# Differential attention's outputs normed by tokens inside its turns, the last layer's splits moved into the last eight turns, and silu by exponential and logarithm

## What is computed

```python
q, gate, q_mem, g_mem = split(rms_norm(x, pre) @ w_in)        # 768, 768, 256, 256 columns
k, v = split(rms_norm(x, kv_norm) @ w_kv)
# 6 pairs of heads, 8 tiles of 128 queries; keys up to the tile's end
p = softmax(q @ k.T / 8 - slope * dist)                        # two maps of each pair
o = (p[0] - lam * p[1]) @ v                                    # 128 features a pair
o = rms_norm(o, subln) * (1 - lam_init)                        # over the 128 features
y = concat(o * silu(gate), memory_attention(q_mem) * silu(g_mem)) @ w_out
x = x + rms_norm(y, post)
```

## Time and profile before

| | us |
|---|---|
| three runs | 3353.6, 3353.5, 3343.42 (median 3353.5) |
| the profiled execution | 3344.59, span 3343.3 |
| PE busy | 2864.3 (86%) |
| DVE busy | 1715.0 (51%) |
| ACT busy | 986.0 (29%) |
| POOL busy | 686.9 (21%) |

### The profile page before, as it was taken

How to read it: one execution, slowest core, us unless ns; L and a number is a source line. 1 busy time by engine, 2 the same in 40 slices (tenths; PEclk the granted TensorE clock), 3 DMA queues, 4 the chain that set the end, 5 groups by cost and what they waited for, 6 DMA issues and landing times.

```text
span 3343.3 us, 49988 instructions
## 1 busy us (share of the span) xinstructions
PE 2864.3 (86%) x20746; PEld 2296.5 (69%) x20746; DVE 1715.0 (51%) x3034; ACT 986.0 (29%) x1803; POOL 686.9 (21%) x531
## 2 busy tenths in 40 slices
PE   7978878699999999689999867777748899999767
PEld 6765667588888888567888646666627678766545
DVE  3425555544444444666554157777654433377634
ACT  3224444311111111633221211111143222255543
POOL 2112233211011110262111012222212211122123
PEclk9988999899999999899999968998979899999978
DMA  3111032011111111113112100000032201111222
GB/s 105 45 51 39 14 100 65 26 58 50 45 51 51 45 51 50 39 57 94 45 38 64 55 1 3 3 3 3 3 113 76 92 29 44 34 33 35 79 82 76
DMA packets 196450, 162.46 MB, mean 49 GB/s; under 512 B 5200, under 2 KB 173818, under 8 KB 195458
## 3 DMA queue, kind: packets, MB, share of 16 engines
q1 hardware_dynamic: 196226, 159.26, 15.1%
HBM read 137.19 MB, written 22.05 MB: 48 GB/s over the span
## 4 chain that ended last, share of the span: by engine, by line
PE 70%; DVE 16%; ACT 6%; issue 4%; POOL 2%; DMA 2%; SPq 0%; POOLq 0%; DVEq 0%; ACTq 0%
PE ps L721 15%; PE ps L723 14%; PE ps L722 14%; PE ps L2267 5%; PE ps L1836 3%; PE ps L1760 3%; DVE r L686 2%; PE ps L1462 1%; PE ps L1464 1%; PE ps L1463 1%; PE ps L773 1%; ACT r L681 1%; PE ps L1827 1%; PE ps L775 1%; PE ps L774 1%
## 5 line engine op out<-in xcount | busy, mean ns | idle before, releaser
L721 PE MATMUL ps<-r,r 128*128 128x512 f32 (+1 forms) x2304 | 939.7, 408 | 145.5 <-DVE r L686 118.5
L722 PE MATMUL ps<-r,r 128*128 128x512 f32 (+1 forms) x2304 | 911.1, 395 | 0.0
L723 PE MATMUL ps<-r,r 128*128 128x512 f32 (+1 forms) x2304 | 910.6, 395 | 0.0
L721 PEld LDWEIGHTS ps<-r,r 128*128 128x128 f32 x2304 | 444.6, 193 | 280.7 <-DVE r L686 132.1
L667 POOL TENSOR_TENSOR sb<-sb 128x1024 f32<-128x1024 f32 x138 | 281.6, 2046 | 1350.7 <-DMA sb<-in_w_ffn_up 483.5
L722 PEld LDWEIGHTS ps<-r,r 128*128 128x128 f32 x2304 | 445.3, 193 | 93.2 <-issue 6.2
L723 PEld LDWEIGHTS ps<-r,r 128*128 128x128 f32 x2304 | 443.3, 192 | 94.9
L2267 PE MATMUL ps<-sb 64*64 64x64 f32 (+2 forms) x8832 | 299.6, 226 | 120.0 <-DVE sb L2515 31.4
L2267 PEld LDWEIGHTS ps<-sb 64*64 64x64 f32 (+1 forms) x8832 | 278.9, 135 | 150.4 <-issue 100.1
L686 DVE TENSOR_TENSOR r<-sb,r 128x1024 fp32r<-128x1024 f32 x198 | 273.9, 1391 | 190.9 <-ACT r L681 190.5
L681 ACT CAST r<-sb 128x1024 fp32r<-128x1024 f32 x198 | 204.9, 1043 | 229.0 <-POOL sb L667 228.9
(11 more groups left out here) (276 smaller groups left out, 3602.1 us busy)
## 6 DMA issues: line engine op xcount, KB each, us to landing
sb<-in_w_out SPq DMA_DIRECT2D x36, 512.0 KB, 4.0
sb<-in_a_w_in SPq DMA_DIRECT2D x29, 512.0 KB, 4.0
sb<-in_w_ffn_gate SPq DMA_DIRECT2D x22, 512.0 KB, 3.8
sb<-in_w_ffn_up SPq DMA_DIRECT2D x22, 512.0 KB, 3.8
sb<-in_w_ffn_down SPq DMA_DIRECT2D x22, 512.0 KB, 3.5
sb<-in_w_in SPq DMA_DIRECT2D x17, 512.0 KB, 4.0
sb<-in_x SPq DMA_DIRECT2D x16, 512.0 KB, 5.5
xs<-sb SPq DMA_DIRECT2D x4, 2048.0 KB, 9.7
```

The lines of the kernel that those rows point to most:

```text
L721: pe.matmul(self.out, w.hi[:, q, self.cols], hi, start=(q == 0), stop=False)
L722: pe.matmul(self.out, w.hi[:, q, self.cols], lo, start=False, stop=False)
L723: ins = pe.matmul(self.out, w.lo[:, q, self.cols], hi, start=False, stop=(q == w.nk - 1))
```

## The change

The output of a pair and tile now is normed in its turn, with tokens in the partitions: ACT squares it with an accumulator and takes Ln and Exp of the column, DVE multiplies. The weights of the norm (`k.sub`) are applied in the copy after the transpose. SubNorm and the Join are gone. The gates are dealt out by `spread` with other counts; silu is made by Exp, then POOL (at most 1e30, plus 1), then Ln and Exp of the negative, then a product on POOL. The splits of the last layer are put in place 3 of turns 42 to 46 (only feature tile 5 of the second half comes later), all their low parts on POOL, the gates' DMA in place 0 of turn 41 in two halves, and a Prepare at the end of turn 46. DVE takes the first reciprocal after the combination.

```diff
@@ class EvictGate @@
-        dve.scalar_tensor_tensor(self.buf(st), st.out, 0.5, self.r[st.h], ALU.mult, ALU.mult)...
...
-        act.activation(self.gated, self.buf(st), ACT.Tanh).then_inc(*s.stage_tanh.up(st.id))
+        act.activation(self.gated, self.buf(st), ACT.Exp, scale=-1.0).then_inc(*s.stage_exp.up(st.id))
     def pool(self, pool, st):
...
+        pool.wait_ge(*s.stage_exp.at(st.id))
+        pool.tensor_scalar(self.gated, self.gated, 1.0e30, 1.0, ALU.min, ALU.add).then_inc(*s.stage_sum.up(st.id))
+    def inverse(self, act, st):
+        s, k = self.s, self.k
+        act.wait_ge(*s.stage_sum.at(st.id))
+        k.functions(act, LN_EXP_SET)
+        act.activation(self.gated, self.gated, ACT.Ln).then_inc(*s.stage_ln.up(st.id))
+        act.wait_ge(*s.stage_ln.at(st.id))
+        act.activation(self.gated, self.gated, ACT.Exp, scale=-1.0).then_inc(*s.stage_inverse.up(st.id))
+    def gate(self, pool, st):
+        s = self.s
+        pool.wait_ge(*s.stage_inverse.at(st.id))
+        pool.tensor_tensor(self.buf(st), self.buf(st), self.gated, ALU.mult).then_inc(*s.stage_gated.up(st.id))
@@ class SplitHi, SplitLo @@
+    def dve(self, dve):
+        for name, event in self.waits:
+            dve.wait_ge(*s[name].at(event))
+        dve.tensor_tensor(self.src, self.src, self.factor, ALU.mult).then_inc(*s.mixed.up((self.key, self.j)))
+    def act(self, act):
+        act.wait_ge(*s.mixed.at((self.key, self.j)))
+        act.copy(self.hi, self.src).then_inc(*s.hi_of_x.up((self.key, self.j)))
+    def pool(self, pool):
+        pool.wait_ge(*s.hi_of_x.at((of.key, of.j)))
+        pool.tensor_tensor(self.lo, of.src, of.hi.bitcast(F32), ALU.subtract).then_inc(*s.lo_of_x_pool.up((of.key, of.j)))
@@ Attention.steps @@
             if t < last:
                 out += part(Scores, t + 1)
+            if t:
+                out += part(NormOut, t - 1)
             out += fill(t, 0)
@@ class NormOut @@
+    def act(self, act):
+            s4 = of.stat(iq, 0)
+            act.wait_ge(*s.scaled_out.at((of.id, i, iq)))
+            act.activation(of.junk, of.on[:, iq % 2, :], ACT.Square, accum_out=s4[:, 0:1]).then_inc(*s.out_squared.up((of.id, i, iq)))
+            act.wait_ge(*s.out_squared.at((of.id, i, iq)))
+            k.functions(act, LN_EXP_SET)
+            act.activation(s4[:, 1:2], s4[:, 0:1], ACT.Ln, bias=k.eps, scale=1.0 / P).then_inc(*s.out_ln.up((of.id, i, iq)))
+            act.wait_ge(*s.out_ln.at((of.id, i, iq)))
+            act.activation(s4[:, 1:2], s4[:, 1:2], ACT.Exp, scale=-0.5).then_inc(*s.out_rstd.up((of.id, i, iq)))
+    def dve(self, dve):
+            dve.wait_ge(*s.out_rstd.at((of.id, i, iq)))
+            dve.tensor_scalar(o, o, s4[:, 1:2], None, ALU.mult).then_inc(*s.out_normed.up((of.id, i, iq)))
@@ class TurnOut @@
-        act.copy(of.out(i, iq), src).then_inc(*s.out_copied.up((of.id, i, iq)))
+        act.activation(of.out(i, iq), src, ACT.Copy, scale=k.sub if of.diff else 1.0).then_inc(*s.out_copied.up((of.id, i, iq)))
@@ layer_b @@
-    yield from [Ring(k, 2), *att.steps(between(k, prods)), Join(k), Ring(k, 4)]
-    yield from finish_layer(k, 1, stored, SubNorm(k, q, lam.e[0], F))
+    for st, t in spread(k, put, prods, 0, [5, 5, 4, 4, 3, 2, 2, 1] * 4 + [5, 4, 4, 4, 3, 2, 2], True):
+        put(t + 1, 0, GateExp(k, st))
+        put(t + 2, 0, GateProduct(k, st))
...
+    put(last - 6, 0, *fetch)
+    order = [(j, h) for h in range(2) for j in (6, 7, 0, 1, 2, 3, 4)]
+    for n, (j, h) in enumerate(order):
+        put(last - 5 + n * 5 // len(order), 3, his[h][j], los[h][j])
+    put(last - 1, 3, his[0][5], los[0][5])
+    put(last - 1, 3, Prepare(k))
+    yield from [Ring(k, 2), *att.steps(fill), After(k, sp=[("turned_out", (att.id, BT - 1, ST - 1))]), Ring(k, 4)]
...
+    yield from weave(first, (1, [back[0], his[1][5], los[1][5], back[1]]))
@@ spread @@
+    left, due, ends = [(st, q) for st in prods for q in range(st.units())], 0, []
+    for n, count in enumerate(counts):
+        due += count
+        for place, share in ((0, 3), (1, 2), (2, 1)) if count > 3 else ((1, 2), (2, 1)):
+            units = []
+            while left and len(units) < -(-due // share) and (not units or units[0][0] is left[0][0]):
+                units.append(left.pop(0))
+            due -= len(units)
+            if units:
+                st = units[0][0]
+                put(begin + n, place, Part(k, st, [q for _, q in units], act_later))
+                if units[-1][1] == st.units() - 1:
+                    ends.append((st, begin + n))
```

More of the change, by code:

```diff
@@ L1684, in steps @@
             out += fill(t, 3)
-        return out + part(ScaleOut, last) + part(TurnOut, last)
+        return out + part(ScaleOut, last) + part(NormOut, last) + part(TurnOut, last)
     def groups(self, i, iq):
@@ L2657, in dve @@
                                          ALU.add, ALU.add).then_inc(*s.step_dve.up(("headed", i, j)))
[L2660 to L2701, removed]
 class RwkvSetup(Step):
@@ L3129, in finish_layer @@
     yield from weave(first, (1, back[:1]), *by(3, splits[1], 1), (6, back[1:]))
[L3130 to L3139, removed]
+    yield from chain(k, ev, y, acc, second, back=[st.event() for st in back])
 def layer_b(k):
@@ L3190, in layer_b @@
                     ready=lambda i, iq: of_v + [("copied_dve", st[i, h]) for h in range(2) for st in (of_q, of_key)])
-    stored = [(f"dma_stage{j}", prods[j - 2].id) for j in range(2)]
-    yield from [Ring(k, 2), *att.steps(between(k, prods)), Join(k), Ring(k, 4)]
-    yield from finish_layer(k, 1, stored, SubNorm(k, q, lam.e[0], F))
[L3196 to L3204, removed]
-            if units:
[L3206 to L3219, removed]
@@ new lines, in layer_b @@
+    table = {}
+    fill = lambda t, place: table.get((t, place), [])
+    put = lambda t, place, *steps: table.setdefault((t, place), []).extend(steps)
+    last = BT * ST - 1
+    for st, t in spread(k, put, prods, 0, [5, 5, 4, 4, 3, 2, 2, 1] * 4 + [5, 4, 4, 4, 3, 2, 2], True):
+        put(t + 1, 0, GateExp(k, st))
+        put(t + 2, 0, GateProduct(k, st))
+    stored = [(f"dma_stage{j}", prods[j - 2].id) for j in range(2)] + [("linear", prods[-1].id)]
+    mix, gates = k.at(X, KT, S), k.at(k.XL, KT, S)
@@ new lines, in layer_b @@
+    y, acc = k.at(F, KT, S), k.halves(F + 14336)
+    ev = EvictSquares(k, lambda i: y[:, i, :], acc, V["post_norm_2"][:, KT:2 * KT])
+    first, second = two_passes(k, lambda i: columns(k, A["w_out_2"][1], i * P), ev, op)
+    back = [Dma(k, k.x[:, :, span_of(h)], k.scratch["xs"][:, :, span_of(h)], f"dma_back{h}",
+                [k.keep[h].event(), *[("lo_of_x_pool", (keys[h], j)) for j in range(KT)]]) for h in range(2)]
+    norms = [Rsqrt(k, acc[h], acc[h], 4 + h, D, ev.summed(h)) for h in range(2)]
@@ new lines, in layer_b @@
+    adds = [residual(k, h, y=y, r=acc[h], rstd_id=norms[h].id) for h in range(2)]
+    rows = k.at(F + 8192, 4, D)
+    store = [Store(k, i, rows, [("x_added", (adds[i // 4][0].key, KT - 1))] if i % 4 == 0 else []) for i in range(ST)]
+    there = [After(k, pool=[st.event()]) for st in back]
+    yield from weave(first, (1, [back[0], his[1][5], los[1][5], back[1]]))
+    yield from weave(second, (1, [norms[0], there[0]]), *by(2, adds[0], 2), (6, store[:2]), (7, store[2:4]))
+    yield from [norms[1], there[1], *adds[1], *store[4:]]
@@ new lines, in spread @@
+def spread(k, put, prods, begin, counts, act_later):
+    left, due, ends = [(st, q) for st in prods for q in range(st.units())], 0, []
[6 more added lines that the diff above has]
+            due -= len(units)
+            if units:
+                st = units[0][0]
+                put(begin + n, place, Part(k, st, [q for _, q in units], act_later))
+                if units[-1][1] == st.units() - 1:
+                    ends.append((st, begin + n))
+    assert not left, len(left)
+    return ends
```

80 lines of the change are left out of this document (55 added, 25 removed).

## The result

The changed kernel is slower: 3363.3 us (3359.7 to 3371.3, six runs) against 3349.1 of the kernel before (3343.4 to 3353.6, six runs), ratio 1.0048, 95% interval 1.0032 to 1.0063. The profiled execution took 3363.8 with a span of 3362.6, 19.3 more than before. The time lies in the stated range, near its upper end; the sign was wrong: I had forecast a gain. The gain behind the attention came as forecast and a little more; the attention lost 74 us where I had 43.6.

A forecast was written before the change was run, and what follows sets the result against it. PE was taken as filled in the attention (busy 246 of about 268 us), with a 38 us chain behind it. Gains of 50.3 less costs of 43.6 gave 6.7: 3338 us on its own time, 3342 named, range 3316 to 3368.

The forecast's parts named there:

- (e): Products in bank 7: PE waits for evictions where products end in mid-turn; 16 counted, cost 10 us taken (3 to 30).
- (g): Last turns, 42 to 46 and tail: wait for the gates' DMA, splits, rounding of product 1's weights; cost 13.6 us.
- (f): Gates: silu takes three ACT passes instead of one, two ahead of the copies; 9 counted, cost 6 us (0 to 12).
- (a): Behind the last turn: norm, Join, split and POOL wait go, product 0 follows at once; gain 49 us (45 to 54).
- (b): Table loads: Tanh goes, ACT stays in one set, the last Rsqrt loses its load; gain 1.3 us.
- R2: Rival, slower: each of 11 mid-turn ends costs 2.7 us at bank 7's eviction; net +13, 3358 us; chance 0.20.
- (c): Attention: pair 5's 16 units move to pairs 0 to 4, 11 us, less 3 back; cost 8 us (5 to 11).
- (d): NormOut on ACT ahead of the copies, hidden in tiles 0 to 4; 1 us a pair, cost 6 us (0 to 15).
- R3: Rival, slower: POOL's subtractions hold DVE back in turns 42 to 47, +16 us; net +9, 3354 us; chance 0.11.
- R4: Rival: ACT's set lacks Ln or Exp, table loads alternate in the attention, 96 loads, 123 us; 3460 us; chance 0.03.
- R1: Rival: the turns' slack absorbs PE's stops, the gates and the DMA wait; net -27, 3318 us; chance 0.22.

The follow-up runs named there:

- e1_ends: The changed kernel with the gates' units dealt out so that each product ends as the last work of a turn: 3330.0 us, 0.9937 of the kernel before.
- e2_silu: The changed kernel without the gates' Ln and second Exp (values are not silu): 3350.8 us, 1.0003 of the kernel before.
- e7_deal: The kernel before with only the gates' units dealt out by spread with the changed kernel's counts: 3371.8 us, 1.0059 of the kernel before.
- e6_bare: e1_ends without the gates' Ln and second Exp and without NormOut's three activations: 3316.2 us, 0.9885 of the kernel before.
- e10_place3: e5_pair5 with the gates' ACT steps one place earlier, behind the exponentials: 3312.5 us, 0.9882 of the kernel before.
- e4_late: The changed kernel with the sixteen splits behind the last turn and among w_out's first products: 3366.1 us, 1.0048 of the kernel before.
- e9_recip: e5_pair5 with the gates' inverse by a DVE reciprocal in place of Ln and Exp on ACT: 3364.9 us, 1.0045 of the kernel before.
- e5_pair5: e1_ends with Prepare moved to turn 41, gates of tiles 0 to 5 fetched in turn 39, tiles 6 and 7 split last: 3327.3 us, 0.9930 of the kernel before.

## Why the prediction was wrong, step by step
The sum had 43.6 for the attention and got 74; what it had for the rest was right. The missing 30 us lie in (e), some 18, in (g), 9, and in (f), some 4.
- (a) 49 forecast, 53 measured: right. Product 0's matmuls took 0.43 us only up to 3241.1 and 0.23 from 3241.7 on, and the wait for product 2's weights was 3.4 instead of 4. (b) 1.3: right.
- **(e), 10 forecast: the step that failed.** The places, the count of eleven and the price in a heavy tile were right (3.1 forecast, 2.93 waited, turn 9.78). The length of the stops, 16 by my count, was nearly right too: the waits are 18.4 us on PE [the waits above]. Two things were wrong. First, of the 16 I took 10 since "some of it falls into slack". Against e1_ends, in which these waits are gone, PE's idle time is 21.4 longer, and no more than some 5 of it belong to turns 11 and 26: of the 18.4 at most a few us were absorbed. Second, the sum had no term at all for the clock, and the same matmuls took 12.3 longer. Together with the two ACT waits the stops take 33.8 of the attention (e1_ends). The two turns in which products end in succession are some 5.5 of it (e2_silu) and belong to (f); about 28 is left for (e). In the kernel before the same dealing costs less: 28.7 in pairs 0 to 4, less 11 for the moved units if (c) is right, is about 18 (e7_deal). The stops need no new work on ACT, but with it they cost more; why, no run shows.
- So R2 was what happened in kind and in the total: it asks for 17 in (e) for the sign to turn, and gave 30 and 3358 on its own time, against about 28 and 3363.8. Its price per end was not what PE waited: R2 had 2.7 at each end, the eleven waits are 0.7 to 3.1 and 1.7 in the mean. That the total fits is in part luck, since the matmuls at the lower clock make up the difference. With 16 in place of 10 the forecast would have been a gain of 0.7.
- (c), (d), (f): on e1_ends' dealing pairs 0 to 4 take 20.1 more than before (241.7 against 221.6), the moved units, NormOut and the gates together. Of the sum, 11 of (c), 5 of (d) and 6 of (f) fall into these pairs: 22. That total was nearly right. The two turns of products that end in succession, some 5.5, come on top, as e1_ends has none: 25.6, 4 more than forecast. Its split is less sure: e6_bare gives ACT's part as 12.5, and leaves 7.6 for the units where (c) had 11.
- (f), 6 forecast, 9 counted: 7.4 by e2_silu. Its cause was rightly named, the place ahead of the copies (e10_place3). Turn 11, ACT and PE:
```profile
2976.09 0.63 ACT L1059 ACTIVATE sb<-sb 128x512 f32<-128x512 f32 x1
2978.16 0.63 ACT L1046 ACTIVATE sb<-sb 128x512 f32<-128x512 f32 x1 [1.44 <-POOL sb L1064]
2978.70 0.57 ACT L1907 COPY sb<-ps 128x512 f32<-128x512 f32 x1
```
```profile
2979.41 2.05 PE L1894 MATMUL ps<-sb 128*128 128x128 f32 x8 [3.08 <-ACT sb L1907]
```
The copy waits for the next product's Exp, that one for POOL's product, and PE 3.08 us for the copy. I had 2 for it; without the passes the turn is 2.7 shorter.
- (g), 13.6 forecast, the second term that was mis-sized. Pair 5 takes 18.4 more than before, but it has also lost its units: beside e7_deal, whose pair 5 has none either (32.3), it is 22.9, where (g) without its tail and one us of NormOut make 13.9. The tail behind the last combination is 1.4 longer (8.77 to 3237.13, 7.40 before) instead of 0.7. DVE in turns 42 and 46 of the changed kernel:
```profile
3191.32 1.90 DVE L1413 TENSOR_TENSOR sb<-sb 128x512 f32<-128x512 f32 x3 [3.92 <-DMA sb<-gates]
```
```profile
3216.18 1.15 DVE L1858 SCALAR_TENSOR_TENSOR sb<-sb 128x896 f32<-128x896 f32 x1
...
3225.56 1.63 DVE L686 TENSOR_TENSOR r<-sb,r 128x1024 fp32r<-128x1024 f32 x1 [2.06 <-ACT r L681]
...
3228.36 1.28 DVE L1858 SCALAR_TENSOR_TENSOR sb<-sb 128x1024 f32<-128x1024 f32 x1
```
The wait is 3.9 where I had 4.4, turn 46 12.18 where I had 11.4. Mis-sized was the splitting itself, of which 3 was taken as mostly hidden: without it (e4_late) turns 42 to 46 are 14.6 shorter, 10.7 without the wait for the DMA. And as in (e) there was no term for the clock: at a mean of 0.69 PE is busy for 34.4 us in this pair, in e7_deal, at 0.99, for 23.5 with the same work:
```profile
3148.78:3181.07 32.29, 23.51 (x143) 14.99 (x142) 24.04 (x78) 18.05 (x46) 0.00 (x0) 0.99 0.02 8
```
- R3, POOL against DVE: the mechanism is there. Two combinations of pair 5 beside which POOL subtracts take 1.0 us longer, in turns 43 and 45; the first is
```profile
3194.39 1.72 DVE L1858 SCALAR_TENSOR_TENSOR sb<-sb 128x512 f32<-128x512 f32 x1
```
against 0.75 for that size before, and 0.75 again in e4_late, in whose turns POOL subtracts nothing. By the rule of the Trainium skill (SBUF — State Buffer, Who interferes with whom) the second to start waits. These rows agree. With the small instructions ahead of the combinations (L1855, 1.03 to 1.10 instead of 0.22 in three turns) it is 4.4 us in all, not 16.
- R4: no table load in the attention. R1: wrong.
- The expectations were right in direction in all but e4_late (as much came back as went) and e9_recip, where both ends had been named. In size e7_deal came below its range, e10_place3 gained more than I wrote (15 against 5 to 8), and in e5_pair5 the median gained 2.7 where I had 7 to 8.

## What to carry to other kernels
Where the bounding engine is nearly always busy, take a counted stop of it as paid in full: here 18.4 us of stops in pairs that had 15.5 us of idle time before cost at least 16 us of idle time, turns 11 and 26 set aside. A stop can cost more than its length: here the matmuls behind the stops ran in part at the lower clock, and made up a third of the price. Before work is dealt out finely between the steps of a pipeline, look at the buffer it goes through: with one PSUM bank, a product that ends in the middle of a turn makes the next wait for an eviction queued behind that turn's long vector work; in this kernel the same units with their ends at the turns' ends are 33 us faster. And the place of a small step in an in-order queue counts for more than its length: moving the three activations of silu from ahead of the copies to where ACT waits anyway gained 8.8 of at most 12.5 us in pairs 0 to 4.

## What the runs showed of the hardware
A DVE reciprocal of 128x512 float32 takes 3.35 us (e9_recip), a multiplication of the same size 0.69. Of PE's stops at bank 7 in the changed kernel, those of turns 3, 6, 13 and 20 (1.96, 2.93, 3.05 and 2.40 us) were followed within 1.2 us by a fall of the granted clock to its lower level, that of turn 9 (2.31 us) was not. After the stop of turn 6 the clock was 0.72 in the mean over 6 us, in which fourteen value matmuls spanned 3.16 instead of 1.73 us. The clock also fell a few times in the kernel before, which has no such stops (0.96 in its attention).
